# Attention scores from 64 rows in pairs, TensorE matmuls in the stage's first waits, and a chunk loop that scales two chunks ahead, in a three-block transformer kernel

## What is computed

```python
for i in range(2):                                   # attention blocks
    h = rms_norm(x, norm_mix_pre[i]); m = rms_norm(mem, norm_mem[i])
    # 12 heads of 64 over the tokens, 4 heads of 64 over 256 memory rows
    tok = windowed_gqa(q, k, v, sink, t5_table) if i == 0 else neighbourhood_attn(q, k, v, rpb)
    mem_out = memory_attn(qm, mk, mv)                # softmax(q k / 8) v
    x = x + rms_norm(concat([tok, mem_out]) @ w_out[i], norm_mix_post[i])
    h = rms_norm(x, norm_ffn_pre[i])                 # gated feed-forward, 1024 -> 2816 -> 1024
    x = x + rms_norm((silu(h @ w_gate) * (h @ w_up)) @ w_down, norm_ffn_post[i])
# third block, end of the time mix, per head of 64 channels; y comes from a chunked recurrence
y = (y - mean) * rsqrt(var + eps) * gn_w + gn_b
y_rwkv = ((y + bonus) * g) @ w_o
```

## Time and profile before

| | before |
|---|---|
| median of 3 runs | 2464.7 us |
| the profiled execution, its own time | 2464.96 us |
| its span, first to last instruction | 2463.2 us |
| TensorE busy | 2356.3 us (96%) |
| VectorE, ScalarE, GpSimd busy | 1035.0, 903.3, 1027.8 us |
| attention of layer 0 in the trace, scores to the last tile's turn | 124.6 to 217.1 us |
| attention of layer 1 | 762.5 to 847.7 us |
| end of the time mix | 1958.7 to 1984.6 us |
| mean granted TensorE clock | 0.978 of full |

### The profile page before, as it was taken

One profiled execution on the slowest core, in us unless ns is written; L12 is line 12 of the kernel. 1 busy time (PEld: TensorE's weight loads), 2 busy tenths in 40 slices (PEclk: granted clock), 3 DMA queues, 4 the chain that ended last, 5 costly groups with the idle time before them and its releaser, 6 DMA issues.

```text
span 2463.2 us, 40817 instructions
## 1 busy us (share of the span) xinstructions
PE 2356.3 (96%) x17172; PEld 1966.5 (80%) x17172; DVE 1035.0 (42%) x1495; ACT 903.3 (37%) x1531; POOL 1027.8 (42%) x564
## 2 busy tenths in 40 slices
PE   7999999999899999999999999999899989999998
PEld 6878788888787878888877888777889767888886
DVE  6174622211455453221146988257433365322212
ACT  5175422322425643332243232545333244322322
POOL 4442544444545054444463444444100265444443
PEclk9999999999999999999999999999999999999998
DMA  6601333333431023333334333323000322333331
GB/s 168 152 14 35 87 109 97 101 94 94 101 103 44 10 77 94 100 97 92 98 82 126 97 101 102 105 85 103 13 4 4 139 64 74 103 95 95 96 95 65
DMA packets 385798, 210.26 MB, mean 85 GB/s; under 512 B 36415, under 2 KB 378151, under 8 KB 385363
## 3 DMA queue, kind: packets, MB, share of 16 engines
q1 hardware_dynamic: 382499, 196.78, 28.3%
q0 software_dynamic: 2448, 9.70, 1.0%
q10 hardware_dynamic: 672, 1.18, 0.1%
HBM read 196.75 MB, written 12.41 MB: 85 GB/s over the span
## 4 chain that ended last, share of the span: by engine, by line
PE 89%; DVE 3%; POOL 2%; ACT 2%; issue 2%; DMA 0%; ACTq 0%; POOLq 0%; DVEq 0%
PE ps L1917 24%; PE ps L1919 24%; PE ps L1918 24%; PE ps L2308 3%; PE ps L2025 2%; PE ps L2005 2%; PE ps L2295 2%; PE ps L2273 2%; PE ps L2014 1%; POOL x_res L721 1%; PE ps L1876 1%; PE ps L2322 1%; ACT w_hi L827 1%; POOL u_r L787 1%; POOL w_lo L658 0%
## 5 line engine op out<-in xcount | busy, mean ns | idle before, releaser
L658 POOL TENSOR_TENSOR w_lo<-raw,w_hi 128x1024 fp32r<-128x1024 f32 (+2 forms) x344 | 811.0, 2358 | 1041.3 <-ACT w_hi L827 1040.8
L1917 PE MATMUL ps<-h_hi,w_hi 128*128 128x512 f32 x2016 | 800.1, 397 | 36.9 <-ACT h_hi L909 12.9
L1919 PE MATMUL ps<-h_lo,w_hi 128*128 128x512 f32 x2016 | 790.3, 392 | 0.0
L1918 PE MATMUL ps<-h_hi,w_lo 128*128 128x512 f32 x2016 | 790.2, 392 | 0.0
L827 ACT ACTIVATE w_hi<-raw 128x1024 fp32r<-128x1024 f32 (+2 forms) x344 | 356.8, 1038 | 1166.2 <-PE ps L1919 1165.3
L1917 PEld LDWEIGHTS ps<-h_hi,w_hi 128*128 128x128 f32 x2016 | 382.4, 190 | 134.6 <-issue 47.2
L1919 PEld LDWEIGHTS ps<-h_lo,w_hi 128*128 128x128 f32 x2016 | 381.8, 189 | 81.6
L1918 PEld LDWEIGHTS ps<-h_hi,w_lo 128*128 128x128 f32 x2016 | 382.6, 190 | 79.0 <-issue 1.2
L1917 PE MATMUL ps<-hid_hi,w_hi 128*128 128x512 f32 x528 | 205.4, 389 | 0.0
L1918 PE MATMUL ps<-hid_hi,w_lo 128*128 128x512 f32 x528 | 205.4, 389 | 0.0
L1919 PE MATMUL ps<-hid_lo,w_hi 128*128 128x512 f32 x528 | 205.4, 389 | 0.0
(11 more groups left out here) (328 smaller groups left out, 2791.8 us busy)
## 6 DMA issues: line engine op xcount, KB each, us to landing
raw<-in_w_gu SPq DMA_DIRECT2D x88, 512.0 KB, 3.9
raw<-in_w_in SPq DMA_DIRECT2D x56, 512.0 KB, 3.9
raw<-in_w_down SPq DMA_DIRECT2D x32, 448.0 KB, 3.8
raw<-in_w_out SPq DMA_DIRECT2D x24, 512.0 KB, 4.1
raw<-in_ffn_w_gate SPq DMA_DIRECT2D x22, 512.0 KB, 3.9
raw<-in_ffn_w_up SPq DMA_DIRECT2D x22, 512.0 KB, 4.0
raw<-in_w_in_b SPq DMA_DIRECT2D x20, 512.0 KB, 3.9
raw<-in_w_down SPq DMA_DIRECT2D x16, 512.0 KB, 4.1
```

Source lines behind the costliest of these rows:

```text
L658: nc.gpsimd.tensor_tensor(lo[:, k0:, :], src[:, k0:, :], hi[:, k0:, :].bitcast(f32), ALU.subtract).then_inc(lo_done, 1)
L1917: nc.tensor.matmul(bank, wh[:, k, :], ah[:, 0:width], start=first, stop=False)
L1918: nc.tensor.matmul(bank, wl[:, k, :], ah[:, 0:width], start=False, stop=False)
L1919: return nc.tensor.matmul(bank, wh[:, k, :], al[:, 0:width], start=False, stop=end)
```

## The change

Three edits in one.

1. *Scores from 64 rows, in pairs.* `q_wide` and all that makes it is gone. The scores contract over the 64 rows that hold the head: rows 0 to 63 for `e` = 0, rows 64 to 127 for `e` = 1, of queries and keys alike. Units run block by block with the two heads beside one another, and TensorE's loop takes two units a turn: scores i and i + 1, transposes i - 3, values i - 5, transposes i - 2, values i - 4. Scores now have four PSUM banks in place of three, transposes two in place of three. In layer 0 heads pair as they lie in `qT` (h and h + 3), so the rows of the output weights are loaded in that order: each panel of `out0` by five DMAs in place of one.
2. *TensorE kept busy.* After the first pair of scores of a layer one float32 matmul of 128 x 128 x 512 into an unused bank, after the second pair three.
3. *Scaling two chunks ahead.* VectorE's order at the end of the time mix is scale(0), scale(1), gate(0), scale(2), and then low(c), gate(c + 1), scale(c + 3).

```diff
--- before.py
+++ after.py
@@ -176,7 +176,6 @@
         qT = at("qT", [P, 6, TOK], big)
         kT = at("kT", [P, 6, TOK], big + 12288)
 
-        q_wide = at("q_wide", [P, 2, KD, TOK], h_off)
         qmT = at("qmT", [P, 2, TOK], big + 24576)
         vtok = at("vtok", [P, 5, HEADS * HD], big + 28672)
         bias_a = at("bias_a", [P, HEADS, SPAN_A], big + 44032)
...
@@ -289,7 +288,12 @@
         dense(linear("k0", 2), wa, 768, 2)
         dense(linear("v0", 2), wa, 1024, 2)
         dense(linear("qm0", 2), wa, 1280, 2)
-        dense(linear("out0", 3), t["w_out"][0], 0, KD)
+        l = linear("out0", 3)
+        for c in range(KD):
+            w = t["w_out"][0][:, c * P:(c + 1) * P]
+            heads_of = w[0:HEADS * HD, :].rearrange("(g e j p) n -> g e p j n", g=2, e=2, j=3)
+            l.panels.append(Panel((heads_of[0], heads_of[1], w[HEADS * HD:D, :].rearrange("(k p) n -> p k n", p=P)),
+                                  KD, by_side=True))
         ffn_linears("0", 4, t["w_gu"][0], 0, t["w_gu"][0], FF, t["w_down"][0])
         dense(linear("q1", 5), wb, 0, 6)
         dense(linear("k1", 5), wb, 768, 6)
...
@@ -343,24 +347,21 @@
         def units(layer):
             lst = []
             for tile in range(8):
-                for e in range(2):
-                    for blk in range(NT):
+                for blk in range(NT):
+                    for e in range(2):
                         u = {"tile": tile, "e": e, "blk": blk, "sink": None, "bias": None}
-                        u["q"] = q_wide[:, e, tile, blk * P:blk * P + P]
+                        rows = slice(HD * e, HD * e + HD)
                         if tile >= 6:
-                            b = 64 * e
-                            u["from"] = (e, qmT[:, tile - 6, :])
-                            u["k"] = mkT[:, layer, tile - 6, :]
+                            u["q"] = qmT[rows, tile - 6, blk * P:blk * P + P]
+                            u["k"] = mkT[rows, layer, tile - 6, :]
                             u["w"] = MEM
                             vc = ((tile - 6) * 2 + e) * HD
                             u["v"] = [(i * P, P, mv[:, layer, i, vc:vc + HD]) for i in range(2)]
                         elif layer == 0:
-                            head = 2 * tile + e
-                            par, i = (head // 3) % 2, (head // 6) * 3 + head % 3
-                            b = 64 * par
+                            head = 6 * (tile // 3) + 3 * e + tile % 3
                             lo_k, hi_k = max(0, blk - 1), min(NT, blk + 2)
-                            u["from"] = (par, qT[:, i, :])
-                            u["k"] = kT[:, i // 3, lo_k * P:hi_k * P]
+                            u["q"] = qT[rows, tile, blk * P:blk * P + P]
+                            u["k"] = kT[rows, tile // 3, lo_k * P:hi_k * P]
                             u["w"] = (hi_k - lo_k) * P
                             c0 = (lo_k - blk + 1) * P
                             u["bias"] = bias_a[:, head, c0:c0 + u["w"]]
@@ -369,10 +370,9 @@
                             u["v"] = [((i2 - lo_k) * P, P, vtok[:, i2, vc:vc + HD]) for i2 in range(lo_k, hi_k)]
                         else:
                             head = 2 * tile + e
-                            b = 64 * e
                             s0, s1 = max(0, P * blk - 64), min(TOK, P * blk + 192)
-                            u["from"] = (e, qT[:, tile, :])
-                            u["k"] = kT[:, tile, s0:s1]
+                            u["q"] = qT[rows, tile, blk * P:blk * P + P]
+                            u["k"] = kT[rows, tile, s0:s1]
                             u["w"] = s1 - s0
                             c0 = s0 - (P * blk - 64)
                             ty = 0 if blk == 0 else (2 if blk == NT - 1 else 1)
...
@@ -401,7 +401,7 @@
 
         loaded_at, count = [], [0] * 4
         for p, pan in enumerate(panels):
-            count[p % 4] += 32 if pan.split else 16
+            count[p % 4] += 80 if pan.by_side else 32 if pan.split else 16
             loaded_at.append(count[p % 4])
         lora = L["lora"]
         PAIRED = ("gu0", "q1", "gu1", "lora", "rwkv_out", "gu2")
...
@@ -622,7 +622,13 @@
                                          [[n_rpb - 1, 16], [31, HEADS * 8], [1, 32]])
                                  ).then_inc(sg["rpb_loaded"], 16)
                 dst = raw[:, p % 4, 0:pan.kc, :]
-                if pan.split:
+                if pan.by_side:
+                    for e in range(2):
+                        for g in range(2):
+                            sp.dma_start(dst[64 * e:64 * e + 64, 3 * g:3 * g + 3, :], pan.src[g][e]
+                                         ).then_inc(loaded[p % 4], 16)
+                    sp.dma_start(dst[:, 6:KD, :], pan.src[2]).then_inc(loaded[p % 4], 16)
+                elif pan.split:
                     sp.dma_start(dst[:, :, 0:64], pan.src[0]).then_inc(loaded[p % 4], 16)
                     sp.dma_start(dst[:, :, 64:128], pan.src[1]).then_inc(loaded[p % 4], 16)
                 else:
...
@@ -687,21 +693,7 @@
                         w = ul[i]["w"]
                         nc.gpsimd.tensor_copy(score[:, i % 4, w:w + 1], ul[i]["sink"]).then_inc(sg["sink_put"], 1)
 
-                def widen(tile):
-
-                    for e in range(2):
-                        b, src = ul[8 * tile + 4 * e]["from"]
-                        ins = nc.gpsimd.tensor_scalar(q_wide[:, e, tile, :], src, head_ones[:, 64 * b:64 * b + 1], None, ALU.mult)
-                    ins.then_inc(sg["q_wide_ready"], 1)
-
-                pool.wait_ge(used, last_reader[2 if layer == 0 else 5])
-                for g in range(L[f"qm{layer}"].g0 + L[f"qm{layer}"].groups - 4, L[f"qm{layer}"].g0 + L[f"qm{layer}"].groups):
-                    freed(pool, g)
                 for i in range(NU):
-                    if i == 4:
-                        widen(1)
-                    if i % 8 == 4 and i // 8 + 2 < 8:
-                        widen(i // 8 + 2)
                     put_sink(i)
 
             added = [0]
...
@@ -945,14 +937,6 @@
                 b0 = NU * layer
                 ul = U[layer]
 
-                def widen_first(e):
-
-                    b, src = ul[4 * e]["from"]
-                    for g in range(L[f"qm{layer}"].g0 + L[f"qm{layer}"].groups - 4, L[f"qm{layer}"].g0 + L[f"qm{layer}"].groups):
-                        freed(act, g)
-                    nc.scalar.activation(q_wide[:, e, 0, :], src, ACT.Copy, scale=head_ones[:, 64 * b:64 * b + 1]
-                                         ).then_inc(sg["q_first"], 1)
-
                 def out_of(i):
 
                     u = ul[i]
...
@@ -962,11 +946,11 @@
                     nv = len(u["v"])
                     rows = [m for _, m, _ in u["v"]]
                     if all(m == P for m in rows):
-                        last = nc.scalar.activation(pT[:, i % 3, 0:nv * P], ps[:, 3 + i % 3, 0:nv * P], ACT.Copy)
+                        last = nc.scalar.activation(pT[:, i % 3, 0:nv * P], ps[:, 4 + i % 2, 0:nv * P], ACT.Copy)
                     else:
...
@@ -984,7 +967,7 @@
                         act.wait_ge(sg["o_norm"], 8 * layer + u["tile"] - 1)
                     act.wait_ge(sg["max_done"], b0 + i + 1)
                     if u["bias"] is None:
-                        nc.scalar.activation(score[:, b, 0:u["w"]], ps[:, i % 3, 0:u["w"]], ACT.Exp,
+                        nc.scalar.activation(score[:, b, 0:u["w"]], ps[:, i % 4, 0:u["w"]], ACT.Exp,
                                              bias=row_max[:, b:b + 1], accum_out=total
                                              ).then_inc(sg["exp_done"], 1)
                     else:
...
@@ -1444,11 +1427,6 @@
                                             h_hi[:, tile, :].bitcast(f32), ALU.subtract).then_inc(hl, 1)
 
                 dve.wait_ge(used, last_reader[2 if layer == 0 else 5])
-                for g in range(L[f"qm{layer}"].g0 + L[f"qm{layer}"].groups - 4, L[f"qm{layer}"].g0 + L[f"qm{layer}"].groups):
-                    freed(dve, g)
-                side0, src = ul[0]["from"]
-                nc.vector.tensor_scalar(q_wide[:, 0, 0, :], src, head_ones[:, 64 * side0:64 * side0 + 1], None, ALU.mult
-                                        ).then_inc(sg["q_first"], 1)
                 sinks_put = 0
                 for i, u in enumerate(ul):
                     b = i % 4
...
@@ -1810,14 +1788,16 @@
             dve.wait_ge(sg["y_scaled"], 1)
             dve.wait_ge(sg["bonus_ready"], 1)
             link(nc.vector.tensor_tensor(u_r[:, 0, :], u_r[:, 0, :], u_v[:, 0, :], ALU.add))
+            scale_y(1)
             gate_y(0)
+            scale_y(2)
             for c in range(KD):
-                if c + 1 < KD:
-                    scale_y(c + 1)
                 low_of_y(c)
                 if c + 1 < KD:
                     dve.wait_ge(sg["y_bonus"], c + 1)
                     gate_y(c + 1)
+                if c + 3 < KD:
+                    scale_y(c + 3)
 
```

(52 more changed lines are left out.)

47 lines of the change are left out of this document (18 added, 29 removed).

## The result

The changed kernel takes 2438.55 us (median, 2436.49 to 2443.85; the executions of the kernel before beside them have a median of 2464.38). The ratio is 0.990, 95% interval 0.988 to 0.992: 26 us less. Five rounds on another chip gave 2438.72 us (2438.31 to 2438.96) and a ratio of 0.990 (0.988 to 0.991). The forecast was 2447 us, range 2438 to 2465. The profiled execution took 2439.93 us, its span is 2438.1, its mean granted clock 0.982.

The account below looks back on a forecast made before the run. TensorE was taken as the bound, busy 2356.3 of 2463.2 us. Steady attention 11.8, layer 0's start 2.1, layer 1's start 1.2 and the chunk loop 2.8 sum to 17.9 us off 2464.96: 2447 us, range 2438 to 2465.

Parts of the forecast that it names:

- Two row groups stream at once: Attention scores: the two heads of a pair stream in the time of one, 0.43, 0.64 or 0.32 us by width.
- the prediction's rival: Attention scores: lone pairs do not overlap, costing 28.2 us, time 2475.3 us; chance 0.12.
- three slots: Attention scores: only the middle two of a pair's four instructions overlap, adding 14.1 us, time 2461.2 us; chance 0.18.
- A visit to 64 rows: TensorE in attention: entering 64-row work and returning costs 0.39 us, bounds 0.33 and 0.50.
- Layer 0's tiles: Attention, layer 0: five token tiles, each 1.06 us shorter, 5.3 us in all.
- Memory tiles: Attention, two in each layer: four pairs of width 256, each tile 0.64 us shorter, 2.6 us in all.
- Layer 1's tiles: Attention, layer 1: five tiles, each 0.46 us less from pairs and 0.33 from merging two visits, 2.3 and 1.6 us.
- Start of layer 0: Attention start: VectorE no longer waits for the fifth sink behind GpSimd's widening; 2.1 us gained, between 0.5 and 3.
- Start of layer 1: Attention start: TensorE, itself late, gets from first transposes to unit 8's scores sooner at full clock; 1.2 us gained.
- Chunk loop: End of the time mix: scaling two ahead removes a wait ring, turns fall from 3.24 to 2.94 us; 2.8 us gained.
- VectorE, GpSimd, SyncE, the five DMAs: Other engines and `out0` panel loads: no cost expected, at most 1 us for the panels where the stage begins.
- the rival on the clock: Start of layer 1: clock falls despite added matmuls, -1.8 in place of 1.2 us, time 2450; within the forecast's 0.70.

Follow-up runs that it names:

- scores apart: Changed kernel with each pair's second score, and the added matmuls behind it, issued after the turn's first transposes and values: 2553.63 us, ratio 1.037.
- the late burst: Changed kernel with its four added matmuls moved from the first two turns of each attention stage to unit 16's turn: 2464.20 us, ratio 0.999.
- four scores in a visit with more cover: Changed kernel with four scores per visit in layer 1's six token tiles, transposes and values one unit later, two added matmuls at unit 4: 2439.71 us.

## Why the prediction was right, and where it was not

The direction and the mechanism held. The gain came out almost half as large again (17.9 us forecast, some 26 measured), and the result stands 0.6 us inside the lower end of a wide range. That it stands inside is partly luck: the range went down to 2438 for visits at 0.33, which came only in part, and for a loop worth 4 at most, which was worth 6.6. Term by term, with the lead of one trace over the other read at the same instructions:

- *Two row groups stream at once*: right, and whole. The kernel with both heads on the same rows puts the overlap at 28.5 us; the prediction's rival had 28.2 for its loss. The same experiment decides the condition of that rival: had it not overlapped, the change would have been worth nothing.
  The Trainium skill (TensorE: Matmul & The Clock Gate, Part 3, The mechanism) says that matmuls keep strict program order in start and end. By that rule as the prediction read it, three slots were to be expected; the pair takes two (0.63 us). In the edge block a score starts at 781.80, ahead of the second instruction (781.94) of the values piece that was issued before it, so across the two row halves the order is not kept as I read it; the measurement decides.
- *A visit to 64 rows*, 0.39 (0.33 to 0.50): measured 0.34 where only visits were added; in layer 0, 2.14 us of streaming and four visits in place of 4.76 us, with the tile 1.14 shorter, give 0.37. A little less than forecast.
- *Layer 0's tiles*: 1.14 us each against 1.06. *Memory tiles*: 0.69 against 0.64. Right.
- *Layer 1's tiles*: 1.11 against 0.46 + 0.33, and the difference is a wait that the prediction did not see, though its row had it (40.79 of 41.16 us busy). Before, TensorE waited once in a tile for VectorE's `normalise`:

```profile
780.51 0.56 PE L2025 MATMUL ps<-vtok,pT 128*128 128x64 f32 x4
781.16 0.42 PEld L1989 LDWEIGHTS ps<-ident,tok_out 128*128 128x128 f32 x4 [0.23 <-DVE tok_out L1437]
```

  From those values to the output transposes it is 0.65 us, and 0.39 now: 0.26 us a tile. The pairs give 0.58, with a visit at 0.36 by the same timelines. Merging the edge block's last values piece with the scores gives some 0.27, where 0.33 was put: such a block with its pair takes 1.11 us from values to transposes (781.52 to 782.63), a plain one 1.12, and the piece by itself had cost 0.24 more than a plain one. That the piece streams beside a score is worth nothing more: with both heads on the same rows, where it can't, a tile is longer by 1.50 us, which is the scores' overlap alone.
- *The last tile*: from its neighbour's output transposes to its own it took 5.50 us and takes 4.37 in each layer. Of the 1.13 some 0.65 is a score and two transposes that now stand ahead of that stretch. The other 0.5 is waits for ScalarE's copies that are gone, 1 us in both layers that no step of the prediction held.
- *Start of layer 0*: unit 8's scores come at 132.44 and came at 136.47, 4.0 less the 1.3 us of lead from before the stage: 2.7 us, where the prediction had 2.6 (before it took off 0.5 for values still owed). Right. Unit 4's maximum came at 129.56, as put (near 130). The experiment with GpSimd kept busy returns 2.2 us of it by the sink alone.
- *Start of layer 1*: by unit 8's scores 1.6 us, as the prediction had it (before it took off 0.4). The first exponential was done near 753.6, which is 764.8 in the time of the trace before (put at 763.6), and the added matmuls held the transposes until 755.26, there 766.5 (put at 766.4); half of them frees 1.3 us.
- *Chunk loop*: 2.8 against 6.6, outside its own bounds. Three errors in one step. The wait at 1983.21 is chunk 6's, not the last one's, so there are seven turns and not six. The turn was worked out as 3.24 x 16.31 / 18.00 from busy time, which holds modelled tails: in TensorE's timeline of the changed kernel the turn is 2.70.

```profile
1952.65 0.79 PE L1897 MATMUL ps<-h_hi,w_hi 128*128 128x512 f32 x1
...
1955.35 0.79 PE L1897 MATMUL ps<-h_hi,w_hi 128*128 128x512 f32 x1
```

  And the last turns have no spread or gate left to issue: they take 2.23, 1.80 and 1.37 us, where each took over 3 before. Had I listed the matmuls of each turn, both would have been seen.
- *VectorE, GpSimd, SyncE, the five DMAs*: nothing, as forecast.

The sum: attention 15.1 forecast, 19.0 in the trace (2.2 of the difference between unit 8 and the end of layer 1's stage); the loop 2.8 and 6.6; together 25.6. The rest of the trace cancels: 1.3 ahead at the outset, 1.2 more before the recurrence, 2.3 lost in it.

The step that was wrong in kind, though the time does not show it, is the rival on the clock. I gave the failing of the added matmuls 3 us (2450). Taking them away costs 9 to 60 us (2447 to 2499). The prediction took the dip's length from the earlier trace rows and the kernel before, which leaves 1.2 GHz by itself after 3.4 and 6.8 us. The changed stage often doesn't: in the one trace of it without them it stays there for 109 us. So the added matmuls are not an accessory worth 3 us but a condition of the whole gain in most executions: without them, and even with the three longest executions left out of it, the ratio to the kernel before is 1.002 (0.999 to 1.004). Three of the twelve still took only 2447 to 2456 us.
The Trainium skill (TensorE: Matmul & The Clock Gate, Why this matters for your kernels) advises keeping TensorE busy continuously and without idle gaps. The wait of 2.39 us in which the fall starts goes the same way. But the kernel with its scores apart falls after 9.40 us without a gap and runs at 0.50 with 82.22 of 82.22 us busy. By that advice taken alone it should have kept full clock; the measurement decides.

What in the stage's work holds the clock down is not shown. What is shown is how long it stayed at 0.50 once it had fallen (scores apart, layer 1: 157 us; paired, layer 1: 109, and 27 until just after the late burst; paired, layer 0: 31, 20.5 and 17; four scores in a visit with more cover: 3.4; unpaired: 7 and 3). That full-size matmuls at the start prevent it in the changed kernel shows in the times: none of the changed kernel's eight executions is long, and all twelve without them are longer than any of these eight.

## What to carry to other kernels

Pairing two 64-row matmuls on opposite row halves streams both in the time of one, but each visit to 64 rows costs 0.34 to 0.37 us. So put several pieces of 64-row work into one visit, and let a neighbouring piece of 64 rows join it. Such a stage may be slow to get its clock back once it has lost it, even while TensorE is busy throughout: fill TensorE's waits at its start with full-size matmuls, look for the clock in the trace after every change of order, and price a stall in it by the stage at half clock and not by its own length. When a ring of waits is removed, count the next engine's instructions turn by turn from start to start, the last turns too, and not from busy time. And where a stretch is not busy to its full length, as in 40.79 of 41.16 us, look for the wait before you price the rest.

## What the hardware showed that I had not expected

- The granted clock can stay at 0.50 (1.2 GHz) for 98 us in which TensorE has no gap (98.00 of 98.00 busy). In one trace it came back 1.1 us into a burst of 128x512 matmuls.
- It can also fall without a gap: at 785.5 with the scores apart, after 9.40 us busy throughout.
- A stall of 2.15 us in TensorE cost 10.8 us: the clock was at 0.50 for 17.1 us after it.
- A 64-row values piece in the same visit as the scores costs nothing over a plain one (1.11 us against 1.12 from values to transposes), and a score starts before the piece is through.
- The recurrence, the same code on the same data, takes 389.4 us at a mean granted clock of 0.97 and 395.6 us at 0.94, and 391.0 or 393.4 us at 0.96.
